# The first eight tiles of a layer projected from x times the norm's vector, the inverse root multiplied when they are taken; squares of the inputs summed by rows

## The chip, the cores and the metric

One Trainium2 chip, one of its cores. The time is the device time of one launch in microseconds (us). Lower is better. The engines are named as in the profile: PE (TensorE, matmuls), PEld (its weight loads), DVE (VectorE), ACT (ScalarE), POOL (GpSimd) and SP (SyncE, which here only issues DMAs).

## The reference

The kernel is one inference step of a two-layer hybrid decoder trunk in float32, for 272 prompt tokens (16 learned ones and 256 given) and 8 sample tokens. These 280 tokens stand side by side in the kernel. What matters here is how a layer begins:

```python
h = rmsnorm(x, w['norm1_g'])      # x * rsqrt(mean(x*x) + 1e-6) * g, per token over 1024 channels
(q_m, k_m, v_m, i_pre, f_pre, o_pre, glu_a, glu_b, q_a, k_a, v_a, g_pre) = split_cols(h @ w['w_in'])
...
u = glu_a * jax.nn.sigmoid(glu_b)
uc, conv_new = causal_dwconv(u, conv_buf, w['w_dconv'], w['b_dconv'])
...
x = x + (g_a * y_a + g_b * y_b + g_c * y_c) @ w['w_out']
h2 = rmsnorm(x, w['norm2_g'])
...                               # gate, up, conv over gate, silu
x = x + (jax.nn.silu(gc) * up) @ w['w_ffn_down']
```

The inverse root is one number per token. So it can be multiplied into h ahead of the projection, or into a projected tile behind it: (x * g * r) @ W is r * ((x * g) @ W), with r the token's inverse root.

## The kernel before

All activations lie transposed in SBUF: channels on the partitions (8 blocks of 128 for the 1024 channels of x, index c or k), 280 tokens in a row. The weights of a layer are cut into 144 pieces, in a fixed order, `PIECES`. Pieces 0 to 3 give the tiles glub 0 to 3 (glu_b), 4 to 7 give glua 0 to 3 (glu_a), 8 is ka, 9 va, 10 to 13 qa, 14 the input and forget gates, then km, vm, qm, o, g, the three branch outputs, out, gate and up, and down at the end. A piece of the input projection is 1024 x 128 weights (512 KB). `n` is a piece's number.

Each piece goes through four engines. SP loads it into one of six slots `w_raw` (line 727) as soon as the piece six places ahead of it has been used (`runs_done`). ACT rounds it to the matmul's reduced format, `w_hi` (`split_hi`, line 1216). DVE subtracts to get the rest, `w_lo` (`split_lo`, line 1639). PE then makes three products for each of 8 blocks k of the contraction (lines 844 to 846): activation hi by weight hi, lo by hi, hi by lo, 24 matmuls of 280 columns a piece. The activations are split into hi and lo in the same way: `h_hi` by ACT (line 1226), `h_lo` by DVE (line 1649).

The order of work on each engine is written out by hand. ACT and DVE both run a loop over n. In iteration n they first take what piece n gave out of PSUM, and then split piece n + 4 (`AHEAD`). Each engine works strictly in this order; semaphores make it wait. The tiles of the input projection go in turn into three PSUM banks, so that PE may begin tile n only when tile n - 3 has been taken. Before, glub tiles are taken by ACT (a sigmoid straight out of PSUM, line 1250) and glua tiles by DVE (a product with that sigmoid, lines 1675 and 1676). The 124 taps of the convolution run on DVE from n = 8 on.

Pieces 0, 1 and 2 are projected as one group (`GROUPS`): PE goes over k, and for each k makes the products of all three, so that it can follow the blocks of h as they come. A layer begins like this:

- The first layer only: x comes in rows of tokens (`x_rows`, five DMAs on one semaphore). PE turns it to channels on partitions, 3 transposes per block c into one bank (lines 746 to 748), DVE copies each block to x (line 1615), ACT squares it (line 1210), and PE sums the squares over the partitions by a product with ones (line 760).
- The second layer: DVE adds each tile of down to x and sums its square (`square`, lines 1626 and 1629), and PE sums over the partitions at the end of the layer (`sum_squares`, line 754).
- Both: ACT takes the root (line 1200), DVE the reciprocal (line 1633), then DVE makes `h_full` = x * g * inverse root block by block (line 1652), ACT rounds it and DVE subtracts (`first_norm` on both engines). PE's wait for piece 0 at each k is for `h_lo`.

Around it, PE turns small vectors (`turn_vectors`, n = 3, lines 777 and 781), the history of the convolution (n = 5, line 854), the new rows of the convolution (n = 8, lines 861 and 862) and the cached keys (n = 9, line 870). SP issues `load_vectors` (12 DMAs) ahead of piece 3 and `load_states` (8 DMAs) ahead of piece 6. The second norm of a layer is already done in another way: gate and up are projected from x * g (`xg_hi`, `xg_lo`), and the inverse root is multiplied into the tiles when they are taken.

Of the kernel before, what the change touches and what calls it, by code (L numbers as in the profile page):

```python
# [24 lines left out]
F32 = mybir.dt.float32  # L25
# [34 lines left out]
BLOCKS = [(0, 128), (128, 128), (256, 16)]  # L60
STACK = 64 + NS
# [135 lines left out]
ON_ACT = ("glub", "ka", "va", "qa", "km", "vm", "qm", "o", "g")  # L197
# [44 lines left out]
def program(nc, ins, outs):  # L242
# [5 lines left out]
    with ExitStack() as ctx:  # L248
# [46 lines left out]
        x_squares = at("x_squares", [P, KD, T], o)  # L295
# [50 lines left out]
        conv_raw = at("conv_raw", [120, NS, P], o); o += TK  # L346
        qm_t = at("qm_t", [P, NH_M, T], o); o += TK
        vm_t = at("vm_t", [P, NH_M, T], o)
        num_all = at("num_all", [P, NH_M, T], o); o += TK
# [45 lines left out]
        tile_banks = ps_tile + work[2:5]  # L395

# [24 lines left out]
        x_in = sem("x_in", 0, 16 * 5)  # L421
# [20 lines left out]
        squares_summed = sem("squares_summed", 4, 2)  # L442
# [27 lines left out]
        x_squared = sem("x_squared", 0, KD)  # L470
        w_hi_ready = sem("w_hi_ready", N_PIECES)
        rms_ready = sem("rms_ready", 2)
# [39 lines left out]
        h_lo_ready = sem("h_lo_ready", 2 * KD)  # L512
        pad_zero = sem("pad_zero", 1)
# [91 lines left out]
        def _(sp):  # L605
            sp.dma_start(const[:, 0:2 * P], consts[:, 0:2 * P]).then_inc(const_in, 16)
            sp.dma_start(x_rows[0:N_META, 0, :], meta).then_inc(x_in, 16)
            sp.dma_start(x_rows[N_META:P, 0, :], x_prompt[0, 0:P - N_META, :]).then_inc(x_in, 16)
            sp.dma_start(x_rows[:, 1, :], x_prompt[0, P - N_META:2 * P - N_META, :]).then_inc(x_in, 16)
            sp.dma_start(x_rows[0:N_META, 2, :], x_prompt[0, SEQ - N_META:SEQ, :]).then_inc(x_in, 16)  # L610
            sp.dma_start(x_rows[N_META:N_META + NS, 2, :], x_sample[:, 0, :]).then_inc(x_in, 16)
            for l in range(DEPTH):
                def load_norm():
                    sp.wait_ge(vec_turned, value("vec_turned", l, 0))
                    sp.dma_start(vec_raw[0:KD, 0, :], norm1_g[l].rearrange("(r p) -> r p", p=P)).then_inc(norm_in, 16)

# [98 lines left out]
                other = {0: [load_norm], 3: [load_vectors], 6: [load_states], 14: [store_conv], 24: [store_kv], 28: [store_m],  # L715
# [21 lines left out]

        @block.tensor
        def _(pe):
            mm, turn = nc.tensor.matmul, nc.tensor.transpose  # L740
            pe.wait_ge(const_in, 16)
            pe.wait_ge(x_in, 16 * 5)
            for c in range(KD):
# [1343 lines left out]
```

## Time and profile before

| | |
|---|---|
| Median of 3 runs | 1139.93 us (1136.01 to 1145.39) |
| Profiled execution | 1137.01 us, span 1135.2 us |
| Granted TensorE clock, mean | 0.958 of full speed |
| PE busy | 1060.4 us (93%) |
| DVE busy | 796.0 us (70%) |
| ACT busy | 536.1 us (47%) |
| Chain that ended last | PE 70%, DVE 17%, ACT 5%, issue 4%, DMA 3% |

How to read it: the span is the stretch of the execution that the profile covers; the profiled execution took 1.8 us more than its span. Busy shares are means over all stages. The chain that ended last is followed back from the last instruction: PE is on it most of the time, and where PE waits, DVE most often. PEclk in a profile is the granted share of TensorE's clock: 1.00 is 2.4 GHz, 0.50 is 1.2 GHz. In the timeline, a row gives start, duration, engine, line, operation and what it writes and reads; matmuls are pipelined, so that the distance from start to start is what one costs and the duration is longer. The same holds for instructions of DVE and ACT that don't wait for each other.

### The profile page before, as it was taken

The numbers are of one execution on the slowest core, as the hardware profiler recorded it, in microseconds if no ns is written. First come the engines' busy times: TensorE is split into PE (matmuls) and PEld (weight loads), VectorE is DVE, ScalarE is ACT, GpSimd is POOL, SyncE is SP. The second block draws the span as 40 slices with busy tenths as digits, with TensorE's granted clock in tenths as the row PEclk, the third lists the DMA queues.
The fourth block names the chain that finished last, engine by engine and source line by source line (L and its number), as shares of the span: only waits on it lengthen the run. The fifth ranks groups of instructions, "written<-read, shape, count | busy, mean of one in ns | idle before, by whom it ended". The sixth has DMA issues, their size and how long they took to land.

```text
span 1135.2 us, 19352 instructions
## 1 busy us (share of the span) xinstructions
PE 1060.4 (93%) x7894; PEld 1002.5 (88%) x7894; DVE 796.0 (70%) x1457; ACT 536.1 (47%) x941; POOL 76.7 (7%) x65
## 2 busy tenths in 40 slices
PE   5999989889898999999979999998998989999997
PEld 3989879778798999999979897896787989999996
DVE  4587986765698677775555889675458868787653
ACT  3545563323834555553334555442175445665432
POOL 0020000313200000000000200011331000000000
PEclk9999999898999999999989999997899989999998
DMA  9654545264445575555576464462454548756561
GB/s 251 156 132 123 131 108 149 60 165 95 140 149 149 148 224 169 173 167 171 158 172 152 127 150 111 113 168 74 112 139 124 151 118 233 208 173 181 174 180 47
DMA packets 318498, 168.21 MB, mean 148 GB/s; under 512 B 25174, under 2 KB 317334, under 8 KB 318218
## 3 DMA queue, kind: packets, MB, share of 16 engines
q1 hardware_dynamic: 318266, 165.83, 53.7%
q8 instruction: 63, 1.03, 0.4%
q10 hardware_dynamic: 144, 1.14, 0.3%
q14 instruction: 25, 0.20, 0.1%
HBM read 160.45 MB, written 9.71 MB: 150 GB/s over the span
## 4 chain that ended last, share of the span: by engine, by line
PE 70%; DVE 17%; ACT 5%; issue 4%; DMA 3%; SPq 0%; DVEq 0%
PE ps_tile L844 14%; PE ps_tile L845 13%; PE ps_tile L846 13%; PE work L844 6%; PE work L846 6%; PE work L845 6%; DVE w_lo L1639 5%; DMA w_raw<-in_w_in 3%; DVE uc L1739 2%; ACT w_hi L1216 2%; PE work L1062 1%; PE work L1064 1%; DVE prod L1690 1%; ACT scores L1341 1%; PE work L1069 1%
## 5 line engine op out<-in xcount | busy, mean ns | idle before, releaser
L1639 DVE TENSOR_TENSOR w_lo<-w_raw,w_hi 128x1024 fp32r<-128x1024 f32 (+1 forms) x288 | 342.9, 1196 | 123.5 <-ACT w_hi L1216 122.9
L1216 ACT ACTIVATE w_hi<-w_raw 128x1024 fp32r<-128x1024 f32 (+1 forms) x288 | 295.2, 1027 | 130.5 <-DMA w_raw<-in_w_ffn_down 67.9
L844 PE MATMUL ps_tile<-h_hi,w_hi 128*128 128x280 f32 (+2 forms) x944 | 286.4, 303 | 10.3 <-DVE h_lo L1649 10.2
L845 PE MATMUL ps_tile<-h_lo,w_hi 128*128 128x280 f32 (+2 forms) x944 | 278.6, 295 | 0.0
L846 PE MATMUL ps_tile<-h_hi,w_lo 128*128 128x280 f32 (+2 forms) x944 | 278.0, 295 | 0.0
L844 PEld LDWEIGHTS ps_tile<-h_hi,w_hi 128*128 128x128 f32 (+1 forms) x944 | 181.7, 193 | 16.8 <-issue 13.8
L845 PEld LDWEIGHTS ps_tile<-h_lo,w_hi 128*128 128x128 f32 (+1 forms) x944 | 181.3, 192 | 1.2
L846 PEld LDWEIGHTS ps_tile<-h_hi,w_lo 128*128 128x128 f32 (+1 forms) x944 | 180.6, 191 | 0.6
L1739 DVE SCALAR_TENSOR_TENSOR uc<-u_pad,vec,uc 128x272 f32<-128x272 f32 x240 | 122.0, 561 | 0.1
L844 PE MATMUL ps_tile<-xg_hi,w_hi 128*128 128x280 f32 (+1 forms) x368 | 108.0, 293 | 7.3 <-DVE x L1696 7.3
L846 PE MATMUL ps_tile<-xg_hi,w_lo 128*128 128x280 f32 (+1 forms) x368 | 107.5, 292 | 0.0
L845 PE MATMUL ps_tile<-xg_lo,w_hi 128*128 128x280 f32 (+1 forms) x368 | 107.4, 292 | 0.0
L844 PE MATMUL work<-xg_hi,w_hi 128*128 128x280 f32 (+1 forms) x336 | 97.6, 291 | 0.0
L846 PE MATMUL work<-xg_hi,w_lo 128*128 128x280 f32 (+1 forms) x336 | 97.6, 290 | 0.0
L845 PE MATMUL work<-xg_lo,w_hi 128*128 128x280 f32 (+1 forms) x336 | 97.5, 290 | 0.0
L1254 ACT ACTIVATE gates<-ps_tile,vec 128x280 f32<-128x280 f32 (+1 forms) x48 | 23.3, 485 | 140.1 <-PE ps_tile L846 140.0
L844 PEld LDWEIGHTS ps_tile<-xg_hi,w_hi 128*128 128x128 f32 x368 | 70.6, 192 | 7.8 <-issue 7.7
L845 PEld LDWEIGHTS ps_tile<-xg_lo,w_hi 128*128 128x128 f32 x368 | 70.5, 192 | 0.1
L846 PEld LDWEIGHTS ps_tile<-xg_hi,w_lo 128*128 128x128 f32 x368 | 70.3, 191 | 0.0
L844 PEld LDWEIGHTS work<-xg_hi,w_hi 128*128 128x128 f32 x336 | 64.0, 190 | 0.3 <-DVE w_lo L1639 0.2
L845 PEld LDWEIGHTS work<-xg_lo,w_hi 128*128 128x128 f32 x336 | 63.8, 190 | 0.0
L846 PEld LDWEIGHTS work<-xg_hi,w_lo 128*128 128x128 f32 x336 | 63.7, 189 | 0.0
(336 smaller groups left out, 1937.1 us busy)
## 6 DMA issues: line engine op xcount, KB each, us to landing
w_raw<-in_w_in SPq DMA_DIRECT2D x98, 512.0 KB, 3.9
w_raw<-in_w_ffn_gate SPq DMA_DIRECT2D x44, 512.0 KB, 3.9
w_raw<-in_w_ffn_up SPq DMA_DIRECT2D x44, 512.0 KB, 3.9
w_raw<-in_w_ffn_down SPq DMA_DIRECT2D x32, 512.0 KB, 3.6
w_raw<-in_w_out SPq DMA_DIRECT2D x16, 512.0 KB, 3.6
w_raw<-in_w_ffn_down SPq DMA_DIRECT2D x14, 384.0 KB, 3.1
w_raw<-in_w_in SPq DMA_DIRECT2D x20, 256.0 KB, 3.7
c_head<-in_state_mlstm_c SPq DMA_DIRECT2D x8, 512.0 KB, 5.5
```

Of the source, the lines that this page charges most:

```text
L844: mm(out, hi[:, k, :], a_hi[:, k0 + k, f:T], start=first, stop=False, skip_group_check=True)
L845: mm(out, hi[:, k, :], a_lo[:, k0 + k, f:T], start=False, stop=False, skip_group_check=True)
L846: m = mm(out, lo[:, k, :], a_hi[:, k0 + k, f:T], start=False, stop=last, skip_group_check=True)
L1062: mm(work[2][:, t0:NP], v[blk], decay_d[0:ns, c:c + nt], start=(blk == 0), stop=(blk == 2))
L1064: m = mm(work[2][:, NP:NP + P + 1], k[blk], v_one[blk], start=(blk == 0), stop=(blk == 2), skip_group_check=True)
L1069: mm(work[4][rows, t0:NP], ones[0:ns, 0:32], decay_d[0:ns, c:c + nt], start=(blk == 0), stop=(blk == 2))
L1216: go(h, r, ACT.Copy).then_inc(w_hi_ready, 1)
L1254: o = go(gates[:, t, f:T], src, ACT.Identity, bias=vcol("b_merge", t))
L1341: go(s, s, ACT.Exp, bias=sm[0:nq, 4 + j:5 + j], accum_out=sm[0:nq, 8 + j:9 + j]).then_inc(unit_exp, 1)
L1639: tt(lo, r, h.bitcast(F32), ALU.subtract).then_inc(w_split[n % SLOTS], 1)
L1690: o = tt(prod[:, t % 2, f:T], src, gates[:, (KD if kind == "yb" else 0) + t, f:T], ALU.mult)
L1739: stt(dst, src, w, dst, ALU.mult, ALU.add).then_inc(tap_done, 1)
```

## The change

1. Pieces 0 to 7 (glub and glua) are projected from `xg` = x * norm1's vector, split into hi (ACT, `first_hi`) and lo (DVE, `first_lo`). The group of pieces 0 to 2 waits for `first_lo`, no longer for `h_lo`. Piece 8 (ka) is now the first that waits for `h_lo`, block by block.
2. h itself is made later: iterations n = 3 to 6 of ACT and DVE make two blocks each of `h_full`, `h_hi` and `h_lo` (the last `h_lo` at n = 7).
3. Taking: a glub tile is taken by DVE (times the inverse root, to `sig_b`), then ACT applies the sigmoid in SBUF. Ahead of taking a glua tile, DVE multiplies the sigmoid by the inverse root.
4. The first layer: x comes on three semaphores; transposes go block of rows by block of rows, into all 8 banks. ACT squares the rows as they come, summing along the row (`accum_out`), and takes two small roots; DVE inverts them and puts them on a diagonal; PE spreads them over the partitions (`spread_row_inverses`, behind the group), and DVE copies the result. The weight splits of pieces 0 to 3 are set between the blocks of x by hand.
5. The second layer: `first_hi` and `first_lo` run in the previous layer's down iterations, as do the splits of the next layer's pieces 0 to 3 (`split_ahead` now crosses the layers). PE sums the squares inside the group, ahead of k = 4.
6. norm1's vector is loaded and turned earlier; `load_vectors` goes from ahead of piece 3 to ahead of piece 4; `turn_vectors` from n = 3 to 5, `turn_conv_history` from n = 5 to 6, and their takes on ACT from 4 to 6 and from 6 to 7.

```diff
-ON_ACT = ("glub", "ka", "va", "qa", "km", "vm", "qm", "o", "g")
+ON_ACT = ("ka", "va", "qa", "km", "vm", "qm", "o", "g")
 ...
# SP
-                other = {0: [load_norm], 3: [load_vectors], 6: [load_states], 14: [store_conv], ...
+                other = {4: [load_vectors], 6: [load_states], 100: [load_next_norm], 14: [store_conv], ...
# PE
+            turn_norm(0)
+            for b, (t0, n) in enumerate(ROW_BLOCKS):
+                pe.wait_ge(x_in[b], 16 * (2, 1, 2)[b])
+                for c in range(KD):
+                    if b == 0 and c == 3:
+                        pe.wait_ge(vec_ready, value("vec_ready", 0, 1))
+                    m = turn(first_banks[c][:, t0:t0 + n], x_rows[0:n, b, c * P:(c + 1) * P], ident[0:n, 0:n])
+                    if b == 2:
+                        m.then_inc(x_turned, 1)
+            def spread_row_inverses():
+                pe.wait_ge(took_dve, KD)
+                for b, (t0, n) in enumerate(ROW_BLOCKS):
+                    pe.wait_ge(diagonal_ready, b + 1)
+                    mm(work[0][:, t0:t0 + n], ones[0:n, 0:P], row_inverse[0:n, b, 0:n], start=True, stop=True)\
+                        .then_inc(inv_rows_spread, 1)
 ...
+                        if pieces[0] == 0 and k == 4 and l > 0:
+                            sum_norm(1, l - 1)
                         for n, out, hi, lo in runs:
+                            if n < 3 and k == 0:
+                                if n == 0 and l == 0:
+                                    pe.wait_ge(took_dve, 3)
+                                pe.wait_ge(w_split[n % SLOTS], value(f"w_split{n % SLOTS}", l, SPLIT_THROUGH[n]))
                             products(n, out, hi, lo, [k], True, True, n == pieces[0])
 ...
                             if n == 0:
+                                pe.wait_ge(first_lo_ready, value("first_lo_ready", l, k + 1))
+                            if n == STEP["ka", 0]:
                                 pe.wait_ge(h_lo_ready, value("h_lo_ready", l, k + 1))
 ...
+                    if n == 0 and l == 0:
+                        spread_row_inverses()
# ACT
+            def first_hi(l, c):
+                if l == 0:
+                    act.wait_ge(took_dve, c + 1)
+                else:
+                    act.wait_ge(took_dve, value("took_dve", l - 1, DVE_NO["down", c] + 1))
+                go(xg_hi[:, c, :], x[:, c, :], ACT.Copy, scale=vcol("norm1", c)).then_inc(first_hi_ready, 1)
+            for b, (t0, n) in enumerate(ROW_BLOCKS):
+                act.wait_ge(x_in[b], 16 * (2, 1, 2)[b])
+                if b > 0:
+                    act.wait_ge(rows_squared, b)
+                go(row_squares[0:n, :], x_rows[0:n, b, :], ACT.Square, accum_out=row_sums[0:n, b:b + 1]).then_inc(rows_squared, 1)
+            ...                                # two roots of 128 x 2 and 24 x 1
+            for c in range(KD):
+                first_hi(0, c)
+                if c in (2, 3, 5, 7):
+                    split_hi(0, (2, 3, 5, 7).index(c))
 ...
+                    if kind == "glub":         # in take
+                        act.wait_ge(took_dve, value("took_dve", l, DVE_NO[tile] + 1))
+                        go(sig_b[:, t, :], sig_b[:, t, :], ACT.Sigmoid).then_inc(sig_ready, 1)
 ...
-                    if n + AHEAD < N_PIECES:
-                        split_hi(n + AHEAD)
+                    split_ahead(l, n)
+                    if 3 <= n < 7:
+                        first_norm_hi(2 * n - 6)
+                        first_norm_hi(2 * n - 5)
# DVE
+            for c in range(3):
+                take_x(c)
+            dve.wait_ge(vec_ready, value("vec_ready", 0, 1))
+            split_lo(0, 0)
+            first_lo(0, 0)
+            take_x(3)
+            first_lo(0, 1)
+            split_lo(0, 1)
+            take_x(4)
+            first_lo(0, 2)
+            take_x(5)
+            first_lo(0, 3)
+            split_lo(0, 2)
+            ...                                # take_x 6, 7, first_lo 4 to 7
+            invert_rows()                      # 2 small reciprocals, 3 diagonals
+            split_lo(0, 3)
+                def invert_first_norm():
+                    if l == 0:
+                        dve.wait_ge(inv_rows_spread, 3)
+                        dve.tensor_copy(rms_inv[:, :], work[0][:, 0:T]).then_inc(rms_inv_ready, 1)
+                    else:
+                        inverse_root(value("rms_ready", l, 1), rms, rms_inv, 0)
 ...
+                    if kind == "glua":         # in take
+                        dve.wait_ge(sig_ready, value("sig_ready", l, t + 1))
+                        tt(sig_b[:, t, :], sig_b[:, t, :], rms_inv[:, :], ALU.mult).then_inc(sig_scaled, 1)
+                        dve.wait_ge(sig_scaled, value("sig_scaled", l, t + 1))
                     tile_ready(dve, l, tile)
+                    if kind == "glub":
+                        o = tt(sig_b[:, t, :], src, rms_inv[:, :], ALU.mult)
 ...
+                        if kind == "down" and l + 1 < DEPTH and t >= 4:
+                            for c in range(4) if t == 4 else (t - 1,):
+                                first_lo(l + 1, c)
+                            if t == KD - 1:
+                                first_lo(l + 1, t)
 ...
+                    split_ahead(l, n)
+                    if 3 <= n < 7:
+                        first_norm(2 * n - 6)
+                        first_norm(2 * n - 5)
+                        for c in range(max(2 * n - 7, 0), 2 * n - 5):
+                            first_norm_lo(c)
+                    if n == 7:
+                        first_norm_lo(KD - 1)
```

## Rows read from the trace of the kernel before

**Rows 1.** The page, busy time, share of the span and instructions of each engine.

```profile
PE 1060.4 (93%) x7894; PEld 1002.5 (88%) x7894; DVE 796.0 (70%) x1457; ACT 536.1 (47%) x941; POOL 76.7 (7%) x65
```

**Rows 2.** Waits of PE: what waited for what, us in total, times, longest.

```profile
PE ps_tile L844 <- DVE h_lo L1649: 10.2, 2, 5.6
```

**Rows 3.** Timeline of the first layer's start: start, duration, engine, line.

```profile
8.37 0.44 PE L746 MATMUL work<-const,x_rows 128*128 128x128 f32 x1 [8.37 <-DMA x_rows<-in_x_sample]
...
9.19 0.47 PE L746 MATMUL work<-const,x_rows 128*128 128x128 f32 x1
...
9.37 0.45 DVE L1615 COPY x<-work 128x280 f32<-128x280 f32 x1 [9.37 <-PE work L748]
...
15.11 5.93 PE L760 MATMUL work<-x_squares,const 128*128 128x280 f32 x16
...
26.02 0.57 PE L844 MATMUL ps_tile<-h_hi,w_hi 128*128 128x280 f32 x1 [4.66 <-DVE h_lo L1649]
```

**Rows 4.** Timeline of PE, first layer: first matmul of piece 3, and of piece 9.

```profile
36.79 0.34 PE L844 MATMUL ps_tile<-h_hi,w_hi 128*128 128x280 f32 x1
...
57.62 0.37 PE L844 MATMUL ps_tile<-h_hi,w_hi 128*128 128x280 f32 x1
```

**Rows 5.** Groups of DVE, first 60 us: busy us, mean ns, idle before.

```profile
L1639 DVE TENSOR_TENSOR w_lo<-w_raw,w_hi 128x1024 fp32r<-128x1024 f32 x13 | 15.7, 1217 | 11.4 <-ACT w_hi L1216 11.4
...
L1633 DVE RECIPROCAL rms_inv<-rms 128x280 f32<-128x280 f32 x1 | 1.9, 1903 | 1.8 <-ACT rms L1200 1.8
L1675 DVE TENSOR_TENSOR u_pad<-ps_tile,sig_b 128x272 f32<-128x272 f32 x4 | 1.8, 440 | 4.6 <-PE ps_tile L846 4.6
...
L1676 DVE TENSOR_TENSOR u_new<-ps_tile,sig_b 128x8 f32<-128x8 f32 x4 | 0.6, 155 | 0.0
```

**Rows 6.** Groups of ACT, first 60 us, same columns.

```profile
L1216 ACT ACTIVATE w_hi<-w_raw 128x1024 fp32r<-128x1024 f32 x13 | 13.6, 1054 | 5.5 <-DMA w_raw<-in_w_in 5.5
...
L1226 ACT ACTIVATE h_hi<-h_full 128x280 fp32r<-128x280 f32 x8 | 3.5, 437 | 4.7 <-DVE h_full L1652 4.7
```

**Rows 7.** Timeline of DVE and ACT: distances from start to start, and a hand-over.

```profile
26.57 0.50 DVE L1652 SCALAR_TENSOR_TENSOR h_full<-x,vec,rms_inv 128x280 f32<-128x280 f32 x1
...
26.99 0.44 DVE L1649 TENSOR_TENSOR h_lo<-h_full,h_hi 128x280 fp32r<-128x280 f32 x1
...
27.35 0.50 DVE L1652 SCALAR_TENSOR_TENSOR h_full<-x,vec,rms_inv 128x280 f32<-128x280 f32 x1
...
36.51 1.05 ACT L1216 ACTIVATE w_hi<-w_raw 128x1024 fp32r<-128x1024 f32 x1
37.46 0.40 ACT L1250 ACTIVATE sig_b<-ps_tile 128x280 f32<-128x280 f32 x1
...
37.60 2.47 DVE L1639 TENSOR_TENSOR w_lo<-w_raw,w_hi 128x1024 fp32r<-128x1024 f32 x2 [4.59 <-ACT w_hi L1216]
```

**Rows 8.** Timeline, layer boundary; last, the first matmuls of pieces 3 and 9.

```profile
573.47 0.45 DVE L1693 TENSOR_TENSOR gate_buf<-work,ffn_rms_inv 128x280 f32<-128x280 f32 x1 [6.14 <-PE work L846]
...
581.56 0.57 PE L844 MATMUL ps_tile<-h_hi,w_hi 128*128 128x280 f32 x1 [5.57 <-DVE h_lo L1649]
...
592.71 0.34 PE L844 MATMUL ps_tile<-h_hi,w_hi 128*128 128x280 f32 x1
...
613.52 0.37 PE L844 MATMUL ps_tile<-h_hi,w_hi 128*128 128x280 f32 x1
```

**Rows 9.** Timeline of PE, the other norm's sum of squares inside a group.

```profile
372.69 1.11 PE L754 MATMUL work<-squares,const 128*128 128x280 f32 x4
```

**Rows 10.** Stretches: busy us (instructions) of PE, PEld, DVE, ACT, POOL; PEclk, DMA share, GB/s.

```profile
581.50:585.50 4.00, 3.94 (x17) 3.97 (x18) 4.00 (x11) 2.19 (x5) 0.00 (x0) 0.50 1.16 256
...
701.90:705.00 3.10, 0.48 (x5) 0.30 (x5) 3.03 (x7) 1.34 (x2) 0.00 (x0) 1.00 0.56 143
705.10:708.40 3.30, 3.30 (x17) 2.42 (x14) 3.20 (x8) 1.76 (x9) 0.00 (x0) 0.50 0.06 16
...
220.40:230.40 10.00, 10.00 (x36) 7.23 (x36) 4.52 (x10) 0.00 (x0) 3.29 (x1) 0.50 0.05 15
```

More of the change, by code:

```diff
@@ L395, in program @@
         tile_banks = ps_tile + work[2:5]
+        first_banks = ps_tile + work
+        row_sums, row_roots, row_invs = small[:, 20:23], small[:, 23:26], small[:, 26:29]
         def con(name, rows=P):
@@ L755, in sum_squares, with sum_norm @@
                     .then_inc(squares_summed, 1)
[L757 to L762 removed]
+            def sum_norm(norm, l):
+                f = first_token(l, "out")
+                sum_squares(0, f, value("squared", l, SQ_STEPS * norm + SQ_STEPS - 1))
+                sum_squares(1, f, value("squared", l, SQ_STEPS * norm + SQ_STEPS))
+            def spread_row_inverses():
[4 more added lines that the diff above has]
+                        .then_inc(inv_rows_spread, 1)
             for l in range(DEPTH):
[L765 to L767 removed]
                 def turn_vectors():
@@ L823, in products @@
                     a_hi, a_lo = {"yb": (conv_hi, conv_lo), "yc": (att_hi, att_lo), "ya": (ml_hi, ml_lo),
-                                  "down": (act_hi, act_lo), "gate": (xg_hi, xg_lo), "up": (xg_hi, xg_lo)}.get(kind, (h_hi, h_lo))
+                                  "down": (act_hi, act_lo), "gate": (xg_hi, xg_lo), "up": (xg_hi, xg_lo),
+                                  "glub": (xg_hi, xg_lo), "glua": (xg_hi, xg_lo)}.get(kind, (h_hi, h_lo))
                     f = first_token(l, kind)
@@ L1212, in _, with root_first_norm @@
             for l in range(DEPTH):
[L1213 to L1226 removed]
+                def root_first_norm():
+                    root_mean((squares_summed, value("squares_summed", l, 0)), D_MODEL, RMS_EPS, work[0][:, 0:T], rms[:, :], rms_ready)
@@ L1228, in second_norm_hi, with first_norm_hi @@
+                def first_norm_hi(c):
+                    act.wait_ge(h_ready, value("h_ready", l, c + 1))
+                    go(h_hi[:, c, :], h_full[:, c, :], ACT.Copy).then_inc(h_hi_ready, 1)
                 def second_norm_hi(c):
@@ L1248, in take @@
                     src = tile_banks[BANK[tile]][:, f:T]
-                    if kind == "glub":
-                        o = go(sig_b[:, t, :], src, ACT.Sigmoid)
-                    elif kind == "o":
+                    if kind == "o":
                         o = go(o_sig[:, t, f:T], src, ACT.Copy)
```

197 lines of the change are left out of this document (108 added, 89 removed).

## The prediction

> **What bounds the kernel now.** I read the busy shares first: PE is busy 93% of the span and DVE 70% [rows 1], so the end moves only where PE waits, or starts to wait. Then the waits of PE: the longest kind is 10.2 us in two pieces, both on `h_lo`, one at the start of each layer [rows 2]. The timelines show the two stretches. In the first layer PE starts its first product at 26.02 [rows 3] and piece 3 at 36.79 [rows 4]. At the boundary down's last tile can be taken at 573.47, PE starts the next group at 581.56 and piece 3 at 592.71 [rows 8]: 8.1 us in which PE does nothing but the sums of squares. Both groups begin at half the clock: 17 matmuls in 4.0 us, where PEclk is 0.50, or 0.235 us each [rows 10]. The group's other 55 take the 7.2 us to 592.71 [rows 8], 0.13 each with a short wait; I take 0.128. From piece 3 to piece 9 lie 20.8 us [rows 4]: 144 matmuls, 18.4, and 2.4 of small turns. So far DVE has little to do there: in the first 60 us it is idle 11.4 us ahead of the weight splits alone [rows 5]. Into this slack the change moves work, so I follow DVE and ACT instruction by instruction until piece 9 starts in each layer; behind that, ACT and DVE wait for PE's pieces as before, and a shift is passed on whole.
>
> **Prices.** One DVE stt of 280 columns costs 0.42 us from start to start, a tensor_tensor 0.36, where nothing is waited for [rows 7]; a dependent one costs its whole duration, 0.44 to 0.50, and about 0.03. A weight split on DVE 1.22 (1.14 unhindered) [rows 5], on ACT 1.05 (0.95) [rows 6, 7]; a sigmoid 0.40; from ACT's end to DVE's start 0.04 (36.51 + 1.05 to 37.60) [rows 7]. From DVE's end to PE about 0.15, an estimate.
>
> **First layer, start.** The rows of x are all there at 8.37 and three transposes cost 0.82 [rows 3], 0.27 each at the mean. Now 8 of each block of rows: the first two blocks start earlier, on their own semaphores (near 5.7, an estimate: the rows land one after another), and end near 9.7; blocks of x are complete from 9.9 on, every 0.2 to 0.27 us, against 0.82 before. That gain is not PE's to keep. DVE's order decides: three copies to 11.2; ACT makes three `first_hi` and split 0 to 12.8; DVE split 0 and `first_lo` 0 to 14.5; only now copy 3, so ACT waits, splits piece 1 to 16.3; DVE to 17.6; copies 4 and 5; ACT splits piece 2 to 20.2; DVE to 21.4. The group needs all three pieces at k = 0, so PE starts in earnest at 21.6, with 66 matmuls to go. It is cold: 3.6 us at 0.235 [rows 10], 51 at 0.128. Group ends at 31.6, not 36.7: **-5.1 us**. The next is late: PE spreads the inverses (three products, 0.8 in all, an estimate from the transposes), DVE copies them (0.45), sets the pad, takes glub 0 (0.45). Piece 3 starts at 33.6, **3.2 us earlier** than before.
>
> **Taking glub.** Bank n - 3 must be free. DVE takes glub n, ACT applies the sigmoid and only then splits n + 4, DVE waits for that and splits, and only then takes glub n + 1: 0.37 + 0.04 + 0.33 + 0.04 + 1.05 + 1.23 = 3.06 us, with hand-overs 3.05 to 3.1, against PE's 24 x 0.128 = 3.08. This just holds: 0.1 us lost. From glub 0's take at 33.0 three such rounds bring the take of glub 3 to 42.1.
>
> **The forgotten queue: h itself.** From here DVE's work of one iteration (n = 4, 5, 6) is: scale the sigmoid 0.48, two parts of the glua take 0.36 + 0.07 and a hand-over [rows 5], weight split 1.14, two `h_full` 0.84, two `h_lo` 0.72: **3.6 us in 3.08 us of PE**. Iteration n = 3 costs 4.4 (it waits for ACT's sigmoid and split ahead of its own), n = 4 3.75 (ACT splits behind its `h_hi`), 5 and 6 3.6 each, n = 7 3.2. So the last `h_lo`, which piece 8 needs at k = 7, is ready at 42.1 + 4.4 + 3.75 + 3.6 + 3.6 + 3.2 = 60.7. PE, let run, would be there at 51. It makes k = 0 to 2 at 51.4, 3 and 4 at 53.8, 5 and 6 at 57.4, and k = 7 at 60.9. Then 0.8 us of turns; piece 9 starts at 62.1, not 57.6 [rows 4]: **first layer +4.5 us**. The queue moved past is DVE's own: `h_lo` stood ahead of the group and stands now behind four weight splits and the glua takes in program order. The weight splits themselves stay in time (piece 12's ends two pieces ahead of its use).
>
> **Second layer.** `first_hi` and `first_lo` for c = 0 to 6 (8 x 0.44 on ACT, 8 x 0.50 on DVE) lie under down's products, where both wait for transfers and PE: cost nothing; if that cover went, 0.5 us a block. Block 7 is ready by 577, PE needs it at 582. PE starts at 573.4; piece 2's raw weights come near 572 (an estimate: its slot comes free with the first third of down's last tile), its split ends at 574.3: 0.25 us of wait. The group is 72 x 0.128 = 9.2 us, at full clock since nothing stopped, and the sums of squares inside it cost 1.0 (1.11 in the other norm [rows 9]). It ends at 583.9, and the root and the reciprocal (1.90 [rows 5]) by 581.7. Piece 3 starts at 583.9, not 592.7: **-8.8 us**. Then the same DVE sequence: 33.6 to 62.1 was 28.5 us, here about 0.7 more, since SP's loads of the states now run into piece 6's load. Piece 9 starts at 613.1, not 613.5 [rows 8]: **-0.4 us**. Of 8.8 us the DVE queue gives back 8.4.
>
> **The clock.** In piece 8 PE works 24 matmuls in 9.7 us. The nearest rows: with 0.48 us busy in 3.1 us, the clock fell and the next 3.3 us ran at 0.50 [rows 10]. I take a fall in both layers and the length of the restart at 581.5: 14 to 17 matmuls at 0.235 instead of 0.128, 1.7 us each: **+3.4 us**. Bounds: nothing, if the full clock stays; 10 us at half, 5 us each, if it lasts as long as 220.4 to 230.4 [rows 10].
> A rule of the Trainium skill bears on this: "TensorE: Matmul & The Clock Gate", section "HAM oscillation — how this bites in real kernels", says that a PE that waits for operands long enough between short bursts is throttled, and starts the next burst cold. Read strictly it asks for one unbroken gap, and my two gaps (54.8 to 57.4, 58.2 to 60.9) are short; by it the sum would have no such term. The row at 701.9 has a gap of this size and a fall, so I keep the term.
>
> SP's order (vectors behind piece 3, norm early) lets piece 3 come 2 us sooner in the second layer and changes no wait of PE. The moved turns are the same products. Row squares: 3 x 1.05 on ACT in place of 8 x 0.44, beside the transfers and PE's turns: nothing; the 16 products with ones go (5.93 [rows 3]), in the -5.1.
>
> **Sum**, against the profiled execution's 1137.0: +4.5 - 0.4 + 3.4 = +7.5, 1144.5. The median of the runs shown lies 2.9 above that execution, so **1147 us**, 0.7% slower.
>
> **Rivals.**
> A. DVE keeps up, and `h_lo` is there when piece 8 needs it (`h_full` spread over slack that I don't see). Then -3.2 and -8.8 stay: 1125 by the execution, 1128 by the median. For it: DVE idle 11.4 us [rows 5]. Against it: the four iterations' sum, of durations that all stand in rows. 0.07.
> B. The same stall, but the clock stays high: 1143.5. 0.15.
> C. The clock decides for slower: PE comes out of piece 8 cold and stays so for 10 us as at 220.4, through pieces 9 and 10, 5 us in each layer: +4.1 + 10 = 1154. It decides if the half clock outlives piece 9. Against it: at 581.5 dense work ended it in 4.0 us; the long stretch had 36 matmuls in 10 us. 0.15.
> Forecast: 0.63.
>
> **Numbers.** A measurement of this kernel can't tell less than 1% (11.4 us) from no change. Faster than 1128.5: only A, and half of what it spreads to, 0.06. Slower than 1151.3: C, and a little of the forecast's upper side (hand-overs 0.1 longer over 20 of them twice are 4 us), 0.19. Same 0.75. Range: B's lower side, with PE's start 3 us sooner in the first layer and the cold stretch hidden, 1137; up to C's middle with 2 us more, 1156; A is left out.
>
> **What would show it.** First product of the group in earnest near 21.6; piece 3 at 33.6; last `h_lo` near 60.7, and a wait of PE on `h_lo` (line of first_norm_lo) of 7 to 8 us in each layer, in parts of 1 to 3 us; PEclk 0.5 around 58 to 64 and again 550 us on; at the boundary no wait above 0.3 us. Wrong if DVE isn't seen busy without a break from 42 to 60, if PE doesn't wait in piece 8, or if the glub rounds take over 3.3 us, which makes it worse.

## The result, and the profile after

| | before | after |
|---|---|---|
| Median of 20 runs each | 1141.93 us (1136.01 to 1149.37) | 1151.91 us (1142.71 to 1160.66) |
| Profiled execution, span | 1137.01, 1135.2 us | 1151.9, 1150.1 us |
| Granted clock, mean | 0.958 | 0.945 |

The ratio is 1.0083, 95% interval 1.0062 to 1.0105: 9.5 us slower, where 7.5 were forecast; the median of 1151.91 us stands against a forecast of 1147, range 1137 to 1156. Two of the changed kernel's 20 executions, over 1.5% above its fastest, count in the median and not in the ratio. The page of the changed kernel, busy time, share and instructions by engine, against [rows 1], and its chain that ended last:

```profile
PE 1066.6 (93%) x7884; PEld 1008.6 (88%) x7884; DVE 812.6 (71%) x1494; ACT 543.2 (47%) x956; POOL 73.6 (6%) x65
...
PE 63%; DVE 20%; ACT 7%; DMA 4%; issue 4%; SPq 2%; DVEq 0%; ACTq 0%
```

PE has ten instructions less and is busy 6 us longer, in keeping with the lower clock. DVE's share of the chain has risen from 17 to 20%. The waits of PE after the change, against [rows 2] (what waited for what, us in total, times, longest):

```profile
PE ps_tile L876 <- DVE h_lo L1769: 10.6, 6, 2.6
...
PE ps_tile L876 <- DVE w_lo L1698: 4.8, 2, 2.8
PE ps_tile L876 <- DVE xg_lo L1692: 4.4, 1, 4.4
```

The wait on `h_lo` was 10.2 us in two pieces ahead of the group. It is now 10.6 us in six pieces, three in each layer, in the middle of piece 8. What was to go has only changed its place and its shape. The waits on `w_lo` and `xg_lo` are those at the start of the first layer (14.96, 17.99 and 21.89).

The timeline of PE in the first layer (start, duration, engine, line, and in brackets the idle time before it and what ended it): the last product that lacked a weight split, the sums of the inverse roots, piece 3, and piece 8 with its three waits and the turns behind it.

```profile
21.89 0.60 PE L876 MATMUL ps_tile<-xg_hi,w_hi 128*128 128x280 f32 x1 [2.83 <-DVE w_lo L1698]
...
32.61 0.93 PE L792 MATMUL work<-row_inverse,const 128*128 128x128 f32 x6
34.73 0.37 PE L876 MATMUL ps_tile<-xg_hi,w_hi 128*128 128x280 f32 x1 [1.19 <-DVE sig_b L1792]
...
54.76 0.40 PE L876 MATMUL ps_tile<-h_hi,w_hi 128*128 128x280 f32 x1 [0.90 <-DVE h_lo L1769]
...
58.36 0.60 PE L876 MATMUL ps_tile<-h_hi,w_hi 128*128 128x280 f32 x1 [2.55 <-DVE h_lo L1769]
...
61.69 0.60 PE L876 MATMUL ps_tile<-h_hi,w_hi 128*128 128x280 f32 x1 [1.57 <-DVE h_lo L1769]
...
62.56 0.41 PE L893 MATMUL work<-const,u_pad 128*30 128x128 f32 x1
```

Piece 3 is 2.1 us earlier than in [rows 4]; the turns behind piece 8 are 5.7 us later (62.56; 56.83 before). The timeline of DVE shows why. First the take of glub 3 with DVE's waits for ACT's split on both sides of it, then the end of its work on h:

```profile
42.11 1.23 DVE L1698 TENSOR_TENSOR w_lo<-w_raw,w_hi 128x1024 fp32r<-128x1024 f32 x1 [1.45 <-ACT w_hi L1244]
43.25 0.44 DVE L1792 TENSOR_TENSOR sig_b<-ps_tile,rms_inv 128x280 f32<-128x280 f32 x1
45.15 1.23 DVE L1698 TENSOR_TENSOR w_lo<-w_raw,w_hi 128x1024 fp32r<-128x1024 f32 x1 [1.45 <-ACT w_hi L1244]
...
54.98 0.44 DVE L1788 TENSOR_TENSOR sig_b<-sig_b,rms_inv 128x280 f32<-128x280 f32 x1
...
58.58 0.44 DVE L1788 TENSOR_TENSOR sig_b<-sig_b,rms_inv 128x280 f32<-128x280 f32 x1
...
60.05 1.23 DVE L1698 TENSOR_TENSOR w_lo<-w_raw,w_hi 128x1024 fp32r<-128x1024 f32 x1 [0.48 <-ACT w_hi L1244]
61.19 0.44 DVE L1769 TENSOR_TENSOR h_lo<-h_full,h_hi 128x280 fp32r<-128x280 f32 x1
```

Two neighbouring scalings of the sigmoid are 3.60 us apart: one iteration of DVE, where PE needs 3.08 for a piece. Behind PE's broken stretch the clock is down (stretches: busy us and instructions of PE, PEld, DVE, ACT, POOL; PEclk, DMA share, GB/s), and the same pieces of work then take longer:

```profile
21.90:26.60 4.70, 4.70 (x20) 4.70 (x21) 4.20 (x12) 3.29 (x4) 0.00 (x0) 0.50 1.17 253
...
57.40:67.60 10.20, 7.68 (x32) 6.73 (x33) 6.28 (x14) 4.73 (x9) 0.00 (x0) 0.50 0.00 0
...
68.90:105.90 37.00, 34.96 (x257) 32.40 (x255) 27.50 (x49) 17.89 (x32) 5.99 (x7) 0.91 0.45 117
105.90:308.50 202.60, 191.24 (x1338) 170.47 (x1337) 139.39 (x262) 88.41 (x183) 27.72 (x15) 0.92 0.47 122
```

The last two stretches are the same work as these two of the kernel before:

```profile
60.80:95.40 34.60, 31.98 (x257) 29.36 (x254) 27.67 (x50) 17.07 (x29) 5.80 (x7) 1.00 0.48 125
95.40:293.70 198.30, 186.98 (x1336) 167.09 (x1336) 139.59 (x262) 87.73 (x185) 27.76 (x15) 0.94 0.48 123
```

Between the traces lie 14.9 us, by the ratio 9.5. The turning of the cached keys, behind piece 9, comes at 68.87 after and 60.78 before: 8.1 us in the first layer. From there to 308.5 another 6.7 us are added (37.0 against 34.6, 202.6 against 198.3), with the same instructions at a lower clock. The first experiment shows below that this part doesn't come of the stall; whether all of it is chance stays open. In the second layer the distance is 14.9 at the boundary (588.23 for the first product of the group, where the kernel before had its last one of down near 573.3 [rows 8]) and 16.3 at the keys (633.03 and 616.69): 1.4 us. Behind them it shrinks to the 14.9 of the end. So 8.1 + 1.4 = 9.5 us lie in the two starts of a layer, as much as the ratio says. That the two agree to the tenth is luck; the profiled execution of the kernel before is 4.9 us under its median, that of the changed one at its median.

### The profile page after: what moved, and what is told of

Read it like the earlier page. It is cut to its first block, busy times and chain, and to the rows that moved or that the text cites. A ratio compares the mean times of both kernels' runs of the same rounds, so it can differ in the third digit from the quotient of the medians.

```text
span 1150.1 us, 19385 instructions
## 1 busy us (share of the span) xinstructions
PE 1066.6 (93%) x7884; PEld 1008.6 (88%) x7884; DVE 812.6 (71%) x1494; ACT 543.2 (47%) x956; POOL 73.6 (6%) x65
## 4 chain that ended last, share of the span: by engine, by line
PE 63%; DVE 20%; ACT 7%; DMA 4%; issue 4%; SPq 2%; DVEq 0%; ACTq 0%
PE ps_tile L876 12%; PE ps_tile L877 12%; PE ps_tile L878 11%; DVE w_lo L1698 7%; PE work L876 6%; PE work L878 6%; PE work L877 6%; ACT w_hi L1244 3%; DMA w_raw<-in_w_in 3%; DVE uc L1863 2%; DMA w_raw<-in_w_ffn_up 1%; PE work L1094 1%; ACT scores L1404 1%; PE work L1096 1%; PE work L1101 1%
## 5 line engine op out<-in xcount | busy, mean ns | idle before, releaser
L876 PE MATMUL ps_tile<-h_hi,w_hi 128*128 128x280 f32 (+2 forms) x816 | 251.7, 308 | 11.4 <-DVE h_lo L1769 10.6
L877 PE MATMUL ps_tile<-h_lo,w_hi 128*128 128x280 f32 (+2 forms) x816 | 243.9, 299 | 0.0
L878 PE MATMUL ps_tile<-h_hi,w_lo 128*128 128x280 f32 (+2 forms) x816 | 243.5, 298 | 0.0
L876 PE MATMUL ps_tile<-xg_hi,w_hi 128*128 128x280 f32 (+1 forms) x496 | 147.7, 298 | 18.7 <-DVE x L1815 7.4
L877 PE MATMUL ps_tile<-xg_lo,w_hi 128*128 128x280 f32 (+1 forms) x496 | 145.9, 294 | 0.0
L878 PE MATMUL ps_tile<-xg_hi,w_lo 128*128 128x280 f32 (+1 forms) x496 | 145.8, 294 | 0.0
L876 PEld LDWEIGHTS ps_tile<-xg_hi,w_hi 128*128 128x128 f32 x496 | 95.8, 193 | 20.9 <-issue 15.0
L877 PEld LDWEIGHTS ps_tile<-xg_lo,w_hi 128*128 128x128 f32 x496 | 95.8, 193 | 0.1
L878 PEld LDWEIGHTS ps_tile<-xg_hi,w_lo 128*128 128x128 f32 x496 | 95.6, 193 | 0.0
L876 PE MATMUL work<-act_hi,w_hi 128*128 128x280 f32 (+1 forms) x220 | 63.7, 290 | 0.0
```

What stands on the lines that cost most here:

```text
L876: mm(out, hi[:, k, :], a_hi[:, k0 + k, f:T], start=first, stop=False, skip_group_check=True)
L877: mm(out, hi[:, k, :], a_lo[:, k0 + k, f:T], start=False, stop=False, skip_group_check=True)
L878: m = mm(out, lo[:, k, :], a_hi[:, k0 + k, f:T], start=False, stop=last, skip_group_check=True)
```

## The experiments

Each was timed in turns with the kernel before. A ratio is to the kernel before; the changed kernel's is 1.0083. "Last h_lo" is the end of the last of the eight, as first layer and second layer.

### h made in the gaps

```diff
 # ACT
-                    if 3 <= n < 7:
-                        first_norm_hi(2 * n - 6)
-                        first_norm_hi(2 * n - 5)
+                    if n < 4:
+                        first_norm_hi(2 * n)
+                        first_norm_hi(2 * n + 1)
 # DVE, between the take and the weight split
+                    if n < 4:
+                        first_norm(2 * n)
+                        first_norm(2 * n + 1)
+                    if 1 <= n < 5:
+                        first_norm_lo(2 * n - 2)
+                        first_norm_lo(2 * n - 1)
                     split_ahead(l, n)
-                    if 3 <= n < 7:
 ...
```

> The changed kernel, but h's blocks are made in iterations 0 to 3 (h_lo to 4), between DVE's take of a glub tile and its weight split, where the changed kernel's DVE idles 1.45 us a round waiting for ACT. Same instructions, other order. Theory (DVE's program order holds h_lo back from piece 8): the last h_lo ends near 48 instead of 61.6, PE has no wait on h_lo above 0.3 us, no half clock near 57 to 67; piece 9 starts at 34.7 + 20.8 = 55.6 (changed 63.4, before 57.6), and in the second layer 8.8 us ahead of before. Time about 11 us under before, ratio 0.990. Rival (the hand-over between DVE and ACT for glub is the limit): each of the 4 rounds grows by what h costs DVE in it (1.56 us), so 6 us come back in each layer: ratio about 1.000. Rival (the clock or something later in the layer made the loss): piece 9 early but the end unmoved, ratio 1.006 or more.

Measured: 1130.9 us median (6 runs), ratio 0.9913 (0.988 to 0.9946). Last `h_lo` 47.86 and 605.36 instead of 61.64 and 626.56, turns behind piece 8 at 54.58 instead of 62.56. PE has no wait on `h_lo` of the first norm left. The timeline of DVE, one glub round of this kernel:

```profile
36.99 0.44 DVE L1792 TENSOR_TENSOR sig_b<-ps_tile,rms_inv 128x280 f32<-128x280 f32 x1
37.35 0.92 DVE L1765 SCALAR_TENSOR_TENSOR h_full<-x,vec,rms_inv 128x280 f32<-128x280 f32 x2
38.19 0.80 DVE L1769 TENSOR_TENSOR h_lo<-h_full,h_hi 128x280 fp32r<-128x280 f32 x2
38.91 1.22 DVE L1698 TENSOR_TENSOR w_lo<-w_raw,w_hi 128x1024 fp32r<-128x1024 f32 x1
40.04 0.44 DVE L1792 TENSOR_TENSOR sig_b<-ps_tile,rms_inv 128x280 f32<-128x280 f32 x1
```

The round is 3.05 us, as before, but the 1.45 us in which DVE waited for ACT's split now hold two blocks of h. The same instructions at another place are worth 1.7%. That is the whole loss of the change and 1% more: the change itself is a gain of 0.9% once h has left the critical stretch.

This kernel also tells whose the later 6.7 us are. Its stretches that match those above:

```profile
58.50:95.50 37.00, 34.95 (x257) 32.47 (x255) 27.73 (x50) 17.84 (x32) 5.99 (x7) 0.91 0.47 117
95.50:298.00 202.50, 191.24 (x1338) 170.52 (x1338) 139.40 (x262) 88.74 (x184) 27.73 (x15) 0.92 0.47 122
```

37.0 and 202.5 us, as in the changed kernel, with no wait on `h_lo` ahead of them. The stall doesn't cause them. (This trace is of the slowest of its six executions, 1138.82 us.)

### h in the gaps, second layer only

The same edit under a condition:

```diff
+                    if l > 0 and n < 4:
+                        first_norm(2 * n)
+                        first_norm(2 * n + 1)
 ...
-                    if 3 <= n < 7:
+                    if l == 0 and 3 <= n < 7:
```

> The changed kernel with h in the gaps in the second layer only; the first layer as in the changed kernel. Theory (the second layer keeps its gain of 8.8 us at piece 3 once h_lo is early; its part of the loss is 7.7 us and 1.5 of clock): the second layer is 8.5 to 9.5 us shorter than in the changed kernel, the first unmoved: ratio 1.0083 - 0.0079 = 1.0004. Rival (the loss sits in the first layer and the second only passes it on): 1.007.

Measured: 1144.85 us (12 runs), ratio 1.0016 (0.9993 to 1.004); last `h_lo` 61.43 and 612.12. The second layer's share is 0.0067, 7.7 us, with an interval of 3.6 us either way; the rest of the 0.017 is the first layer's.

### h for 8 of 280 columns

```diff
-go(h_hi[:, c, :], h_full[:, c, :], ACT.Copy)
+go(h_hi[:, c, 0:8], h_full[:, c, 0:8], ACT.Copy)
-stt(h_full[:, c, :], x[:, c, :], vcol("norm1", c), rms_inv[:, :], ...)
+stt(h_full[:, c, 0:8], x[:, c, 0:8], vcol("norm1", c), rms_inv[:, 0:8], ...)
-tt(h_lo[:, c, :], h_full[:, c, :], h_hi[:, c, :]..., ALU.subtract)
+tt(h_lo[:, c, 0:8], h_full[:, c, 0:8], h_hi[:, c, 0:8]..., ALU.subtract)
```

The other columns of `h_hi` and `h_lo` hold a constant that POOL writes at the start and PE waits for, so this kernel leaves out most of h; its first product of the group in earnest comes at 22.14, 0.25 us later than in the changed kernel.

> The changed kernel with h_full, h_hi and h_lo made for 8 of the 280 columns only (the rest of h is a constant set at the start, so that what is computed from piece 8 on is not the step's): h's 24 instructions a layer stay in their place, at about 0.1 us each instead of 0.4. Theory (DVE's busy time in iterations 3 to 7 is the price): last h_lo near 53, at or ahead of PE's arrival at piece 8 (52), PE waits at most 1 to 2 us, no half clock: ratio 0.991. Rival (the order of glub's takes and the bank waits cost as much): ratio above 1.000 with waits of PE on sig_b or u_new in place of h_lo.

Measured: 1146.01 us (10 runs), ratio 1.005 (1.0022 to 1.0077). My theory missed (0.991 expected). Last `h_lo` ends at 58.43, only 3.2 us sooner. A wait of PE and the end of DVE's work:

```profile
PE ps_tile L877 <- DVE h_lo L1772: 7.0, 4, 2.1
```

```profile
43.66 0.44 DVE L1795 TENSOR_TENSOR sig_b<-ps_tile,rms_inv 128x280 f32<-128x280 f32 x1
...
52.74 0.44 DVE L1791 TENSOR_TENSOR sig_b<-sig_b,rms_inv 128x280 f32<-128x280 f32 x1
...
54.88 0.36 DVE L1768 SCALAR_TENSOR_TENSOR h_full<-x,vec,rms_inv 128x8 f32<-128x8 f32 x2
55.16 0.39 DVE L1772 TENSOR_TENSOR h_lo<-h_full,h_hi 128x8 fp32r<-128x8 f32 x2
55.47 0.45 DVE L1791 TENSOR_TENSOR sig_b<-sig_b,rms_inv 128x280 f32<-128x280 f32 x1
...
57.12 1.22 DVE L1701 TENSOR_TENSOR w_lo<-w_raw,w_hi 128x1024 fp32r<-128x1024 f32 x1 [0.67 <-ACT w_hi L1245]
58.27 0.16 DVE L1772 TENSOR_TENSOR h_lo<-h_full,h_hi 128x8 fp32r<-128x8 f32 x1
```

An iteration is 2.73 us now (52.74 to 55.47), shorter than PE's 3.08, and still PE waits. So the surplus of work per iteration, in which I had seen the cause, is only part of it. The take of glub 3 stands at 43.66, though PE began piece 3 at 35.14 in this kernel and had it done 3.08 later, near 38.2. DVE is 5.4 us behind PE before the first block of h is begun, and at 0.35 us an iteration it makes little of that good. The next two kernels try this.

### ACT splits before it applies the sigmoid

```diff
 # ACT
+                    if n < 4:
+                        split_ahead(l, n)
                     for tile in PIECES[n][4]:
                         if LAST_RUN[tile] < RUNS_THROUGH[n]:
                             take(tile)
-                    split_ahead(l, n)
+                    if n >= 4:
+                        split_ahead(l, n)
```

> In iterations n = 0 to 3 ACT splits piece n + 4 before it applies the sigmoid to glub tile n; DVE's order is the changed kernel's, h included. Theory (a lag): in the changed kernel DVE takes glub 3 at 43.25 though PE had finished it near 37.8. It starts 5 us late, because the first three tiles wait together for the inverse root, and its round of 3.04 us (1.45 of it waiting for ACT's split) is as long as PE's piece, so the lag is never made up; the last h_lo stands behind the take of piece 7 and inherits it. With the split ahead of the sigmoid a round costs DVE 1.5 us, and what limits it is the landing of pieces 6 and 7: take of glub 3 near 38 to 39, its split near 39 to 40, last h_lo near 56 (61.2 before), waits of PE on h_lo 1 to 3 us in a layer instead of 5.3. Ratio to the kernel before 1.000 (changed kernel 1.0083), bounds 0.996 to 1.004. Rival (DVE's sum of work decides, or the landing of the weights): last h_lo within 1.5 us of 61.2 and 1.008.

> The edit of e9 together with that of e4: h is made for 8 of its 280 columns, the rest of h_hi and h_lo holds a constant. e4 alone gave 1.005 and its last h_lo at 58.4, PE waiting 7.0 us. Theory (a lag): with both the DVE keeps up with PE from glub 3 on, the last h_lo comes where DVE has split behind the take of piece 7, near 53 to 54, PE waits for it under 1 us in a layer, the clock stays high there; ratio 0.992, bounds 0.988 to 0.996. Rival (e4's rest is not the lag but something else behind piece 7): within 0.003 of e4's 1.005 less what e9 gains over the changed kernel.

Measured, DVE's order untouched: 1145.62 us (12 runs), ratio 1.0018 (0.9995 to 1.0041). Last `h_lo` 56.40 (56 expected) and 616.94. Together with the short h: 1139.07 us (12 runs), ratio 0.9972 (0.9945 to 1.0), 0.008 under the short h alone; last `h_lo` 53.59 and 614.59. This time is outside the theory's bounds by 0.001, and it is what the rival gave: 1.005 less the 0.0065 that the split first gains is 0.9985, and 0.9972 lies within its 0.003. So the two gains add up, and the times don't tell theory from rival. For the first layer the traces do, and there the lag is shown. With the split first the glub rounds are 1.5 us, DVE takes glub 3 at 39.50 (PE began that piece at 35.56), and one wait of PE is left, of 1.09 us in place of 5.0 in all; with both edits none is. DVE of the kernel with the split first, and then its PE:

```profile
36.46 0.44 DVE L1795 TENSOR_TENSOR sig_b<-ps_tile,rms_inv 128x280 f32<-128x280 f32 x1
36.87 1.23 DVE L1701 TENSOR_TENSOR w_lo<-w_raw,w_hi 128x1024 fp32r<-128x1024 f32 x1
38.01 0.44 DVE L1795 TENSOR_TENSOR sig_b<-ps_tile,rms_inv 128x280 f32<-128x280 f32 x1
...
39.50 0.44 DVE L1795 TENSOR_TENSOR sig_b<-ps_tile,rms_inv 128x280 f32<-128x280 f32 x1
```

```profile
56.46 0.40 PE L876 MATMUL ps_tile<-h_hi,w_hi 128*128 128x280 f32 x1 [1.09 <-DVE h_lo L1772]
```

With the short h on top, DVE waits for PE again, as a sign that it has caught up:

```profile
47.95 0.44 DVE L1800 TENSOR_TENSOR u_pad<-ps_tile,sig_b 128x272 f32<-128x272 f32 x1 [1.11 <-PE ps_tile L879]
```

The second layer keeps its wait, and there the second half of the rival (the landing of the weights) has its part. ACT of the kernel with the split first, from the boundary on:

```profile
590.09 1.04 ACT L1244 ACTIVATE w_hi<-w_raw 128x1024 fp32r<-128x1024 f32 x1
591.08 0.44 ACT L1309 ACTIVATE sig_b<-sig_b 128x280 f32<-128x280 f32 x1
597.58 1.06 ACT L1244 ACTIVATE w_hi<-w_raw 128x1024 fp32r<-128x1024 f32 x1 [6.06 <-DMA w_raw<-in_w_in]
598.54 0.42 ACT L1309 ACTIVATE sig_b<-sig_b 128x280 f32<-128x280 f32 x1
```

SP issues the load of piece 6 at 593.20, right behind its loads of the states (584.38 to 592.8). ACT waits 6.06 us for it with the sigmoid of glub 2 queued behind, and DVE takes glub 3 only behind that. The lag comes back from another side. That is probably also why both edits together fall short of what I expected: in their second layer PE still waits 0.71 and 2.07 us.

### Products that keep PE busy

```diff
                             if n == STEP["ka", 0]:
+                                for _ in range({3: 8, 5: 18, 7: 12}.get(k, 0)):
+                                    mm(work[0][:, 0:T], hi[:, k, :], xg_hi[:, 0, :], start=True, stop=True, ...)
                                 pe.wait_ge(h_lo_ready, value("h_lo_ready", l, k + 1))
```

> The changed kernel with 38 extra products in each layer on PE, ahead of k = 3, 5 and 7 of piece 8 (8, 18 and 12), into a bank nobody reads then: PE is kept busy in the stall, and its end doesn't move. Theory (the stall makes TensorE fall to half its clock and the restart pays for it): last product of piece 8 at the same 62.4, PEclk 1.00 from 57 on, piece 10 comes 2 to 2.5 us earlier than in the changed kernel, in both layers: 4 to 5 us less, ratio 1.004. Rival (the half clock costs nothing that isn't waited for anyway): 1.008, no move.

Measured: 1145.39 us (12 runs), ratio 1.0032 (1.0009 to 1.0056). The stall is as long as in the changed kernel (last `h_lo` 62.23 and 620.07), but 38 products of nothing fill it. Two stretches of this kernel, the stall's end and the 10 us behind piece 9:

```profile
56.00:66.00 10.00, 8.98 (x69) 8.37 (x69) 7.32 (x16) 5.09 (x10) 0.00 (x0) 1.00 0.01 3
66.75:76.75 10.00, 10.00 (x81) 10.00 (x80) 7.18 (x17) 5.40 (x10) 0.00 (x0) 1.00 0.63 152
```

The clock doesn't fall there, nor at 620. By the ratios that is 0.005, 5.8 us of the 9.5, with an interval of 3.6 us either way. The keys come 2.1 us earlier in the first layer (66.75 for 68.87), though the last `h_lo` was 0.6 later.

### The blocks of x copied first

```diff
 # DVE, first layer
-            for c in range(3):
+            for c in range(KD):
                 take_x(c)
 ...
-            take_x(3)
-            first_lo(0, 1)
-            split_lo(0, 1)
-            take_x(4)
 ...
+            for n in range(3):
+                split_lo(0, n)
+                first_lo(0, n)
```

> The changed kernel, but DVE copies all eight blocks of x first, then splits pieces 0 to 2 and makes first_lo. Theory (the group's late start is DVE's order of copies and splits, which makes ACT wait 2.1 and 1.65 us for copies): PE's products in earnest from about 18.0 instead of 21.9, group ends near 28.8, and all that follows is 3.9 us earlier: ratio 1.0083 - 0.0034 = 1.005. Rival (transfers or the transposes set the start): no move, 1.008. Rival (what is gained is lost in the stall at piece 8): no move at piece 9; the theory says it moves by the same 3.9, since h's chain starts at the group's end.

> Both orders together: h's blocks in DVE's gaps of iterations 0 to 3, and all copies of x ahead of the first splits. Theory (two separate losses in DVE's order): positions add up, piece 3 of the first layer at 30.9 and no wait on h_lo anywhere; the first 300 us are 3.7 us ahead of the kernel with h in the gaps alone: ratio 0.9913 - 0.0032 = 0.988. Rival (the earlier start is given back within the layer, as the unmoved ratio of the copies alone could mean): 0.991, with the lead gone by the second layer.

The first was put on the changed kernel: 1149.94 us (6 runs), ratio 1.0082 (1.0055 to 1.0109), where 1.005 was expected: no gain to be seen. On its timeline PE starts the group in earnest 3.9 us sooner, against 21.89 above, and the lead of 3.8 us is still there at the turns behind piece 8 (58.76):

```profile
17.99 0.60 PE L876 MATMUL ps_tile<-xg_hi,w_hi 128*128 128x280 f32 x1 [0.49 <-DVE w_lo L1698]
```

The second adds the copies to the kernel with h in the gaps: 1128.57 us (6 runs), ratio 0.9881 (0.9842 to 0.9919), against 0.9913 for the gaps alone: 3.7 us, the length of the lead. Neither pair of times settles it, for the intervals are as wide as the effect; the positions in the traces do, for the first layer. They don't show that the lead lasts: in the trace of the first of the two, glub 0 of the second layer is taken 1.0 us earlier than in the changed kernel (597.12 for 598.08), so 2.9 of the 3.9 us were lost on the way, behind the first layer's start.

### The inverse roots spread inside the group, and a warm start

```diff
+                        if pieces[0] == 0 and k == 6 and l == 0:
+                            spread_row_inverses()
 ...
-                    if n == 0 and l == 0:
-                        spread_row_inverses()
```

> As the one before, and PE spreads the rows' inverses inside the group of the first layer, ahead of k = 6, not behind it. Theory (behind the group PE waits 1.2 us for DVE's copy and take, beside the 0.9 of the spreading): that wait goes, piece 3 starts 1 to 1.2 us earlier: ratio 0.987. Rival (glub 0's take can't be earlier, since the tile itself closes only 0.8 us ahead of the group's end): less than 0.5 us.

Measured: 1129.47 us (6 runs), ratio 0.9883 (0.985 to 0.9915). In its trace PE doesn't wait for the take of glub 0 any more, and the turns of the vectors come at 38.64 instead of 39.76. The times can't tell it from the kernel without.

The last has 9 products more, in PE's idle time at the start of the first layer (2 on the constants ahead of the first product, 3 and 4 ahead of those that wait for the second and the third weight split):

```diff
                             if n < 3 and k == 0:
                                 if n == 0 and l == 0:
+                                    pe.wait_ge(took_dve, KD)
+                                    for _ in range(2):
+                                        mm(work[4][:, 0:2 * P], ident, const[:, 0:2 * P], ...)
+                                if n > 0 and l == 0:
+                                    for _ in range((0, 3, 4)[n]):
+                                        mm(work[4][:, 0:T], w_hi[0][:, 0:P], xg_hi[:, 0, :], ...)
```

> As the one before, with 9 idle-time products on PE in the first layer's start (2 in float32 ahead of the first product, 3 and 4 ahead of pieces 1 and 2 of the group at k = 0), into a bank that is free. Theory (the clock is at half when the group starts in earnest, because PE did little before; 20 matmuls there cost 0.235 instead of 0.128, 2.1 us): the clock rises sooner, the group ends 1 to 2 us earlier, ratio 0.986. Rival (so few products don't change the granted clock): no gain, and up to 0.6 us lost behind the extra ones, 0.9875.

Measured: 1122.92 us (1122.33 to 1125.01, 5 runs), ratio 0.9839 (0.9813 to 0.9865). It is the fastest of all, 1.6% under the kernel before and 2.4% under the changed one. The stretch from its first product to the spreading of the inverse roots; the changed kernel had 4.7 us at 0.50 in it:

```profile
14.97:23.80 8.83, 8.83 (x62) 8.73 (x62) 6.93 (x15) 4.33 (x6) 0.00 (x0) 0.90 0.97 289
```

In the kernel without the nine, two neighbouring products of the group are still 0.23 us apart at 21.25 and 0.13 from 21.6 on; here they are 0.13 us apart from 16.9 on. But not all of the gain is theirs for certain. The two intervals, 0.985 to 0.9915 and 0.9813 to 0.9865, overlap, and in this trace the first copy of x starts 0.7 us sooner (10.22 for 10.94), ahead of any of the nine.

## Why the prediction was right, and where a size was off

**Start of the first layer, -5.1 us at the group's end.** The order of DVE was right: 21.89 for 21.6. The group ended at 32.6, 1.0 later than forecast, and -4.1 us came of it. That is the first mis-sized term. 0.3 of it is the later start; some 0.5 is the cold stretch, in which 20 products (21.89 to 26.49) stood 0.23 us apart, where the sum had 15, in 3.6 us; the row that it names [rows 10] shows 17, in 4.0 us. The rest is rounding. Piece 3 then followed in 2.1 us, where 2.0 were worked out.

**Glub rounds.** 3.0 us by the takes (34.20, 37.18, ..., 43.25), 3.05 to 3.1 forecast. The take of glub 3 is late by the 1.1 us of the late start.

**The queue of h.** From that take to the last `h_lo` 18.6 us were forecast and 18.4 measured (43.25 to 61.64). Iterations of 3.60 us came as worked out. PE's waits in piece 8 are 0.90, 2.55 and 1.57 us, 5.0 in the first layer and 5.6 in the second; I had said 7 to 8 in each, and the prediction's own times give 7.2 (piece 8 from 51 to 61.3, less 3.08). PE began piece 8 only at 52.47, 1.5 us later, with the last `h_lo` 0.9 later; and the burst of k = 5 and 6 (58.36 to 60.1) ran at half the clock and filled 0.9 us of a wait. From 46 to 61 DVE was never idle for more than 0.48 us. By the letter one of the signs of being wrong did come, for from 42 to 60 it isn't busy without a break: it waits 1.45 us ahead of 45.15. The 4.4 us for n = 3 had that wait in them; the sign was put too strictly.

**What I had wrong in it is the reason.** The prediction sets the iterations' 3.6 us against PE's 3.08 and makes that surplus the price. The short h took the surplus away, and 3.2 us of the delay went with it. The rest is the lag with which DVE enters iteration 3, about 5.4 us, as the first layers of the two kernels with the split first show. It arises where three tiles wait for one inverse and each glub round of DVE is as long as PE's piece, as DVE and ACT wait for each other in turn. The sum contained it (the take at 42.1 was worked out), but the text didn't name it, and so took the wrong operation for the dear one.

**Second layer, -8.8 and -0.4 us.** Piece 3 starts at 598.68; with the distance of 14.9 at the boundary that is -8.9. The turns behind piece 8 come at 627.47, 14.7 behind those before, so -0.2; 0.4 of this is the clock under the last three products, which leaves -0.6. The last `h_lo` at 626.56 undid the whole lead, as forecast. At the boundary PE has no wait above 0.2 us; 0.25 was forecast.

**The clock, +3.4 us.** It fell in both layers, at 57.4 and 624.0. From the product that had waited for the last `h_lo` to the turning of the keys PE takes 4.5 us at full clock (62.28 to 66.75 in the kernel with the 38 products), 7.2 in the changed kernel's first layer (61.69 to 68.87) and 6.4 in its second (626.61 to 633.03). So the clock cost 2.7 and 1.9 us, against 1.7 each: the second mis-sized term. In the first layer the half clock lasted 10.2 us from 57.4 and reached into piece 9. Rival C said 10 us in each layer. The first layer's length was that, but it had put the start behind piece 8: 4.3 us of it lay ahead of the last `h_lo`, where a slow PE costs nothing. In the second layer it was 6.8 us (624.0 to 630.8). The Trainium skill, "TensorE: Matmul & The Clock Gate", section "HAM oscillation — how this bites in real kernels", read strictly asks for one unbroken gap. The trace agrees with its mechanism and not with that reading: the clock fell at 57.4, behind a wait of 0.90 us, six products and 1.6 us of the next wait, and the row at 701.9, kept against that reading, was the better guide.

**Sum.** 8.1 + 1.4 = 9.5 us against 7.5 (6.2 in the first layer, 1.3 in the second): 1.0 too little for the group's late end and 1.0 for the clock, both in the first layer. The median lies 4.9 above the forecast of 1147: 2.0 of that is the kernel before, whose median is 1141.93 over 20 runs and was 1139.93 over 3. Rival A (DVE keeps up, 1128) is what the kernel with h in the gaps does, at 1130.9; it needed another order, not faster work. Rival B (the stall with a high clock, 1143.5) is what the 38 products made, at 1145.39. Both numbers hold within 3 us.

**Left open.** The half-clock stretches between 69 and 308 us cost the changed kernel and that with h in the gaps 6.7 us against the one trace of the kernel before. The other traces show how much this part of the program varies. From the turning of the keys in the first layer to the sums of squares of its second norm, the kernel before takes 311.9 us (60.78 to 372.69), the changed kernel 318.2 (68.87 to 387.06), and its ten variants, whose edits all take effect ahead of it, 313.0 to 321.4. A difference of 6 us between two single traces is thus within what these traces differ by. But the one trace of the kernel before lies under all eleven others, by 1.1 us at least, and is 4.9 under its own median, so it isn't settled whether a part of the 6.7 us is the change's.

## What to carry to other kernels

When work is moved to a later place in an engine's queue, ask first how far behind that engine is when it gets there, and only then how much work it is. A round that two engines pass to and fro, as long as the bound engine's own step, keeps every delay it starts with; the idle time inside such a round is the place for the moved work. A stall on the engine that bounds the kernel costs again in the clock, so where it can't be removed it may pay to fill it.

## What the runs showed of the hardware that was not expected

- A DVE operation on 128 x 8 costs a third of one on 128 x 280 and not a thirty-fifth: two `h_full` take 0.28 us from start to start (54.88 to 55.16) where two full ones take 0.84 (37.35 to 38.19).
- 9 products in PE's idle time at the start come with 5 us less (0.9883 to 0.9839, intervals that overlap). The positions account for 2.0 at the keys (53.68 to 51.66), of which 0.7 lie ahead of the nine, and 4.9 at the turning of the sample scores (91.12 to 86.21), where a later half-clock stretch is also gone.
- The spread of a program's executions differs by program: 18 us over 20 runs of the changed kernel, 12.7 us over 6 of the one with h in the gaps, 2.7 us over 5 of the one with the warm start. No run tells why.
